# Output projection in units of 512 columns, from weight blocks of half the channel blocks

## The reference, cut to what matters

```python
h   = layer_norm(x) * (1 + sc1) + sh1
# mixer: attention and SSD branches, then
merged = sigmoid(g_a) * (attn @ w_attn_o) + sigmoid(g_b) * (y @ w_ssd_o)
mix    = merged @ w_out                       # the output projection: 640x1024 @ 1024x1024
x  = layer_norm(ALPHA * x + g1 * mix, ln1_g, ln1_b)
h  = layer_norm(x) * (1 + sc2) + sh2
ff = square(relu(h @ w_mlp1 + b_mlp1)) @ w_mlp2 + b_mlp2
x  = layer_norm(ALPHA * x + g2 * ff, ln2_g, ln2_b)
```

## Time and profile before

| | us |
|---|---|
| median of 3 runs | 1561.07 (1559.13 to 1561.4) |
| the profiled execution's own time | 1560.75 |
| its span, first to last instruction | 1559.1 |
| output projection on PE, from its first matmul to its last one's start | 1055.96 to 1115.27 |
| PE's wait before the MLP | to 1118.15 |

### The profile page before, as it was taken

One profiled execution on the slowest core, in us unless ns is written; L12 is line 12 of the kernel. 1 busy time (PEld: TensorE's weight loads), 2 busy tenths in 40 slices (PEclk: granted clock), 3 DMA queues, 4 the chain that ended last, 5 costly groups with the idle time before them and its releaser, 6 DMA issues.

```text
span 1559.1 us, 25181 instructions
## 1 busy us (share of the span) xinstructions
PE 1502.1 (96%) x10114; PEld 1394.2 (89%) x10114; DVE 1021.0 (65%) x1407; ACT 689.6 (44%) x1258; POOL 220.5 (14%) x230
## 2 busy tenths in 40 slices
PE   4999999999999989899999999999999999999997
PEld 2899999999999989898866799999998898998986
DVE  5666666658565688988876453346966773653768
ACT  2443343343564266777766443233532262451540
POOL 1011122100101100000000000000000541522720
PEclk9999999999999999999999999999999999999999
DMA  9555555543677777787630355335212122131241
GB/s 317 181 177 192 180 184 184 181 138 112 211 247 243 270 222 223 256 262 226 221 125 1 115 183 169 132 115 190 95 55 82 54 94 97 55 102 61 82 175 68
DMA packets 152511, 244.62 MB, mean 157 GB/s; under 512 B 8112, under 2 KB 110240, under 8 KB 149344
## 3 DMA queue, kind: packets, MB, share of 16 engines
q1 hardware_dynamic: 129232, 174.59, 33.5%
q0 software_dynamic: 12304, 47.72, 8.4%
q10 hardware_dynamic: 10880, 20.97, 5.2%
HBM read 196.63 MB, written 46.63 MB: 156 GB/s over the span
## 4 chain that ended last, share of the span: by engine, by line
PE 78%; DVE 13%; ACT 5%; DMA 1%; issue 1%; SPq 1%; ACTq 0%; DVEq 0%
PE acc L965 57%; PE tp L965 17%; ACT arena L1922 2%; DVE wlo L2288 1%; PE tp L1432 1%; DVE arena L2562 1%; DMA arena<-in_w_mod 1%; PE tp L1093 1%; DVE arena L2393 1%; ACT whi L1700 1%; DMA arena<-decay_sums_t 1%; DVE arena L2563 1%; ACT whi L2080 1%; DVE wlo L2763 1%; PE tp L1479 1%
## 5 line engine op out<-in xcount | busy, mean ns | idle before, releaser
L965 PE MATMUL acc<-hh,whi 128*128 128x322 f32 (+1 forms) x1068 | 287.0, 317 | 5.0 <-issue 3.0
L965 PE MATMUL acc<-hl,whi 128*128 128x322 f32 (+1 forms) x1068 | 280.6, 311 | 0.0
L965 PE MATMUL acc<-hh,wlo 128*128 128x322 f32 (+1 forms) x1068 | 279.9, 311 | 0.0
L965 PEld LDWEIGHTS acc<-hh,whi 128*128 128x128 f32 x1068 | 188.2, 189 | 9.7 <-issue 7.3
L965 PEld LDWEIGHTS acc<-hl,whi 128*128 128x128 f32 x1068 | 189.6, 189 | 0.0
L965 PEld LDWEIGHTS acc<-hh,wlo 128*128 128x128 f32 x1068 | 189.4, 189 | 0.0
L965 PE MATMUL acc<-whi,hh 128*128 128x256 f32 x640 | 183.1, 286 | 0.0
L965 PE MATMUL acc<-whi,hl 128*128 128x256 f32 x640 | 179.8, 281 | 0.0
L965 PE MATMUL acc<-wlo,hh 128*128 128x256 f32 x640 | 179.7, 281 | 0.0
L2288 DVE TENSOR_TENSOR wlo<-raw,whi 128x2048 fp32r<-128x2048 f32 x62 | 145.0, 2338 | 35.2 <-ACT whi L1700 35.2
L1700 ACT ACTIVATE whi<-raw 128x2048 fp32r<-128x2048 f32 x62 | 118.3, 1908 | 71.4 <-PE tp L965 48.3
(11 more groups left out here) (366 smaller groups left out, 3137.9 us busy)
## 6 DMA issues: line engine op xcount, KB each, us to landing
raw<-in_w_in SPq DMA_DIRECT2D x38, 1024.0 KB, 8.8
raw<-in_w_mlp SPq DMA_DIRECT2D x32, 1024.0 KB, 5.2
arena<-in_w_mod SPq DMA_DIRECT2D x24, 1024.0 KB, 8.3
arena<-decay_sums_t ACTq DMA_DIRECT2D x40, 512.0 KB, 6.0
arena<-xs_nat SPq DMA_DIRECT2D x8, 1024.0 KB, 10.7
raw<-in_w_ssd_o SPq DMA_DIRECT2D x8, 1024.0 KB, 6.6
y_nat<-arena POOLq DMA_DIRECT2D x6, 1024.0 KB, 7.5
arena<-y_nat SPq DMA_DIRECT2D x6, 1024.0 KB, 6.6
```

The costliest lines, as they stand in the source:

```text
L965: return pe.matmul(out, l, r, start=first, stop=last)
```

## The change

`w_out` comes in four blocks of 4 channel blocks by 512 columns, of the same 1024 KB (`wide` gives the view of a slot in that form). A unit is a tile by 512 columns, `OUT` lists (tile, column half, offset, columns), and `OUT_BANK` the `acc` bank. There are 11 units: tiles 0, 1 and 2 by the first column half, run as two passes over four channel blocks each; the same tiles by the second half; tile 3 and tile 4 by both, the last unit in two parts of 256 columns. `TURN` has tile 0 after unit 5, tile 1 after unit 7, tile 2 after unit 9. The first MLP block's split waits for unit 8, the last that uses `whi`.

```diff
-        U_MLP = U_OUT + 4 * NT
+        N_OUT = 2 * NT + 1
+        U_MLP = U_OUT + N_OUT
...
-        TURN = {10: 0, 14: 1, 17: 2}
+        OUT = [(t, 0, 0, 2 * BW) for t in range(3)] + [(t, 1, 0, 2 * BW) for t in range(3)]
+        OUT += [(3, 0, 0, 2 * BW), (3, 1, 0, 2 * BW), (4, 0, 0, 2 * BW), (4, 1, 0, BW), (4, 1, BW, BW)]
+        OUT_BANK = (0, 1, 2, 3, 0, 1, 2, 3, 0, 1, 3)
+        TURN = {5: 0, 7: 1, 9: 2}
...
-            stream(2, w_out, 0)
+            for c in range(2):
+                for b in range(2):
+                    step(lo)
+                    sp.wait_ge(lo["sem"], value(lo, 2))
+                    sp.dma_start(wide(raw, b), w_out[:, b * HK:(b + 1) * HK, c * 2 * BW:(c + 1) * 2 * BW]).then_inc(raws[b]["sem"], step(raws[b]))
...
+            def out_products(i, b):
+                t, c, at, n = OUT[i]
+                wh, wl = (wide(w, b) for w in ((whi, wlo), (w2h, w2l))[c])
+                for k in range(HK):
+                    kk = b * HK + k
                     if i == 0:
-                        pe.wait_ge(s["merge_ok"], k + 1)
...
+                        pe.wait_ge(s["merge_ok"], kk + 1)
+                    for m, w in ((hh, wh), (hh, wl), (hl, wh)):
+                        last = mul(acc[:, OUT_BANK[i], 0:n], m[:, kk, tok(t):tok(t) + P], w[:, k, at:at + n],
+                                   kk == 0 and w is wh and m is hh, kk == KT - 1 and m is hl)
                 return last
...
+            for b in range(2):
+                pe.wait_ge(lo["sem"], due(lo))
+                for i in range(3):
+                    if b == 0:
+                        step(free)
+                        pe.wait_ge(s["acc_free"], U_OUT - 1 + i // 2)
+                    last = out_products(i, b)
+                    if b:
+                        last.then_inc(ready["sem"], step(ready))
+            for i in range(3, N_OUT):
                 step(free)
...
+                pe.wait_ge(s["acc_free"], U_OUT + (0, 1, 2, 3, 4, 5, 6, 8)[i - 3])
+                for b in range(2):
+                    if i == 3:
+                        pe.wait_ge(lo["sem"], due(lo))
+                    last = out_products(i, b)
+                last.then_inc(ready["sem"], step(ready))
                 if i in TURN:
                     turn_tile2(TURN[i])
...
-                    act.wait_ge(ready["sem"], U_OUT + 17)
+                    act.wait_ge(ready["sem"], U_OUT + 9)
                     split_hi(0)
...
-                    act.wait_ge(ready["sem"], U_OUT + 18)
+                    act.wait_ge(ready["sem"], U_OUT + 9)
                     split_hi(1)
...
-            gated_out(4)
+            gated_out(1)
             summed(0)
-            gated_out(1)
             normed_once(0)
             gated_out(1)
             normed_twice(0)
             summed(1)
+            normed_once(1)
             gated_out(1)
-            normed_once(1)
-            gated_out(2)
             for t in range(2, NT - 1):
                 lower(t - 2)
                 normed_twice(t - 1)
                 summed(t)
-                gated_out(2)
+                gated_out(1)
                 normed_once(t)
-                gated_out(2 if t == 2 else 1)
+                gated_out(1)
             lower(2)
             split_lo(0)
             gated_out(1)
```

More of the change, by code:

```diff
@@ L436, in build @@
         GATED = {8 + 2 * q: q for q in range(4)}
-        OUT = [(0, 0), (1, 0), (2, 0), (0, 1), (1, 1), (0, 2), (0, 3), (1, 2), (1, 3), (2, 1), (2, 2), (2, 3)]
-        OUT += [(t, b) for t in range(3, NT) for b in range(4)]
-        TURN = {10: 0, 14: 1, 17: 2}
+        OUT = [(t, 0, 0, 2 * BW) for t in range(3)] + [(t, 1, 0, 2 * BW) for t in range(3)]
+        OUT += [(3, 0, 0, 2 * BW), (3, 1, 0, 2 * BW), (4, 0, 0, 2 * BW), (4, 1, 0, BW), (4, 1, BW, BW)]
+        OUT_BANK = (0, 1, 2, 3, 0, 1, 2, 3, 0, 1, 3)
+        TURN = {5: 0, 7: 1, 9: 2}
         LAST = [(t, c, 0, 2 * BW) for t, c in ((0, 0), (1, 0), (2, 0), (3, 0), (0, 1), (1, 1), (2, 1), (3, 1), (4, 0))]
@@ L1501, in _ @@
                     t_pass(1, sub, sub, yh, yl, KT, False, True).then_inc(ready["sem"], step(ready))
-            blocks = [(whi[:, 0], wlo[:, 0]), (whi[:, 1], wlo[:, 1]), (w2h[:, 0], w2l[:, 0]), (w2h[:, 1], w2l[:, 1])]
             def turn_tile2(t):
@@ L1511, in turn_tile2 @@
                 last.then_inc(s["h2_turned"], 1)
-            def out_products(i, ks):
-                t, b = OUT[i]
-                for k in ks:
+            def out_products(i, b):
[3 more added lines that the diff above has]
+                    kk = b * HK + k
                     if i == 0:
-                        pe.wait_ge(s["merge_ok"], k + 1)
-                    for m, w in ((hh, 0), (hh, 1), (hl, 0)):
-                        last = mul(acc[:, i % 4, 0:BW], m[:, k, tok(t):tok(t) + P], blocks[b][w][:, k],
-                                   k == 0 and w == 0 and m is hh, k == KT - 1 and m is hl)
-                return last
@@ L1523, in out_begun @@
[L1523 to L1527, removed]
-                step(free)
[L1529 to L1536, removed]
@@ L1537, in _ @@
-            for i in range(2, 4 * NT):
-                out_begun(i, seen)
-                out_products(i, range(KT)).then_inc(ready["sem"], step(ready))
+                        pe.wait_ge(s["merge_ok"], kk + 1)
+                    for m, w in ((hh, wh), (hh, wl), (hl, wh)):
+                        last = mul(acc[:, OUT_BANK[i], 0:n], m[:, kk, tok(t):tok(t) + P], w[:, k, at:at + n],
+                                   kk == 0 and w is wh and m is hh, kk == KT - 1 and m is hl)
+                return last
@@ L1664, in _ @@
                 if n < 2:
-                    pe.wait_ge(s["acc_free"], U_OUT + 4 * NT - 3 + 2 * n)
+                    pe.wait_ge(s["acc_free"], U_OUT + (9, 7)[n])
                 if n == 3:
@@ L1671, in _ @@
                 if n == 2:
-                    pe.wait_ge(s["acc_free"], U_OUT + 4 * NT)
+                    pe.wait_ge(s["acc_free"], U_MLP)
                     turn_tile2(NT - 1)
@@ L2836, in gated_out @@
                 for i in range(units["k"], units["k"] + n):
-                    t, b = OUT[i]
-                    cols = slice(b * BW, (b + 1) * BW)
+                    t, c, at, n_ = OUT[i]
+                    cols = slice(c * 2 * BW + at, c * 2 * BW + at + n_)
                     dve.wait_ge(ready["sem"], due(ready))
-                    dve.tensor_tensor(x1[:, t, cols], acc[:, i % 4, 0:BW], g1r[:, min(t, 1), cols], ALU.mult).then_inc(free["sem"], step(free))
+                    dve.tensor_tensor(x1[:, t, cols], acc[:, OUT_BANK[i], 0:n_], g1r[:, min(t, 1), cols], ALU.mult).then_inc(free["sem"], step(free))
                 step(units, n)
```

## The result

| | before | changed |
|---|---|---|
| median of 20 runs, us | 1561.07 (1559.13 to 1565.54) | 1563.62 (1562.74 to 1565.84) |
| ratio, 95% interval | 1 | 1.0017 (1.0012 to 1.0023) |
| span of the profiled run, us | 1559.1 | 1561.9 |
| from the start of the output projection on PE to the turning of tile 2 | 52.88 | 55.23 |
| ... to the first matmul of the MLP | 62.19 | 64.52 |

The changed kernel is 2.55 us slower, where 2.4 were forecast. The last three rows are distances in us within one trace, since the stage starts at 1056.30 in the changed kernel's and at 1055.96 in that of before.

The account below looks back on a forecast made before the run. PE's matmul stream was taken to bound the kernel; matmuls -0.71, fourth-block wait +0.3 and cover lost behind tile 2's turning +2.83 gave +2.4 us on 1561.07, so 1563.5 us, range 1561.0 to 1565.4.

Parts of the forecast that it names:

- The matmuls: Output projection on PE: 216 wide matmuls replace 432 narrow ones, 55.93 us for 56.64, a gain of 0.71 us.
- The start: First passes of the output projection: second block's low part is ready in time, new load form costs nothing, no wait.
- The fourth block: Unit 3: low part queued on DVE behind three evictions; PE stops 0.37 plus 0.1 us, net +0.3 us.
- The end of the stage: Tile 2 turned 2.4 us later, same 9.31 us of links, PE waits 5.4 us instead of 2.6 before the MLP.
- the lost cover: Behind tile 2's turning PE has one narrow unit instead of two, so the wait grows by 2.83 us.
- DVE in time: DVE's layer norms from summed(0) to lower(2) need 38.1 us, leaving 0.3 to 0.4 us of slack before the MLP.
- The clock: half_unit(0) after the wait: low clock costs some 1.7 us before; the same cost was taken for the changed kernel.
- the low clock lasts longer: Rival, half_unit(0) and half_unit(1): clock recovers later after the 5.4 us wait; +3.7 us, 1564.8 us; chance 0.28.
- The 0.9: Up to tile 4's turning: the shift is 2.4 - 0.9 us if the low clock falls wholly into the longer wait.
- The sum: Whole kernel: +2.4 us on the median 1561.07 gives 1563.5 us, 0.15% slower.

Follow-up runs that it names:

- e_width_fill: Changed kernel with each 512-column matmul issued as two of 256 and the wait before the MLP filled with 34 added matmuls; +2.05 us over before.
- e_low_fill: Changed kernel with the fourth block's low part on DVE ahead of unit 2's eviction, and 35 added matmuls filling the wait; +0.55 us over before.
- b_turn18: Kernel before with tile 2 turned after unit 18 instead of 17; +3.45 us over before.
- e_turn8: Changed kernel with tile 2 turned after unit 8 instead of 9; +2.61 us over before.
- e_low: Changed kernel with the fourth block's low part on DVE ahead of the eviction of unit 2 instead of behind it; +2.95 us over before.
- b_fill: Kernel before with 17 unused matmuls of 320 columns added between unit 19 and half_unit(0) to fill the wait; -1.27 us against before.
- b_best: Kernel before with the MLP's first four half units running high-part products first, turnings reordered, second block's low part later on DVE; -1.27 us against before.
- a_pool: Changed kernel with the first two MLP blocks' low parts on GpSimd, first high part earlier on ACT, fourth block's low part before unit 2's eviction; +3.63 us over before.
- b_pool: Kernel before with the first two MLP blocks' low parts on GpSimd instead of DVE and the first block's high part earlier on ACT; +2.48 us over before.

## Why the prediction was right

By its own steps. **The matmuls:** a gain of 0.71 us forecast, 0.81 to 0.83 measured by e_width_fill. **The start:** no wait for the second block, as forecast, and none for the first in its new form: PE's timeline has no pause from the end of the work before until unit 3. **The fourth block:** a stop of 0.47 forecast, 0.46 in the trace, and e_low_fill gives it back. The forecast's 0.37 is 0.05 more than its own times 1075.51 and 1075.83 give; in the trace PE did start 0.06 us behind the end of the low part. **The end of the stage:** tile 2 is turned 2.35 us later for 2.4 forecast, the links behind it take 9.29 us for 9.31, the wait is 5.42 for 5.4. b_turn18 gives the same wait by the order alone, so the lost cover, and not the new form of the units, makes it. **DVE in time:** 0.3 to 0.4 us of slack forecast, 0.18 in the trace, since DVE needed 38.26 us from summed(0) to the end of lower(2) (1079.98 to 1118.24) and not 38.1. e_turn8 confirms that there was no more: with the turning 1.38 us sooner the start gained 0.29. This was the step with least room. With another 0.2 us on DVE the number would have been right all the same, but by another chain. **The clock:** taken as unchanged. In the result's profile it was (5.01 us for half_unit(0) and 5.12 before). In general it isn't: longer low stretches are seen after the longer wait, and e_low's half_unit(0) of 6.34 us is what the rival "the low clock lasts longer" had named (6.4). Which of the two the median would follow the forecast had only weighed (0.50 against 0.28), so that it came to +2.55 and not to the rival's +3.7 is in part luck. The cost of the low clock in half_unit(0) before was forecast as 1.7 us and is 1.54 by b_fill (5.12 less 3.58). Of it 1.06 us was said to be all that the turning of tile 4 could come sooner; b_fill gained 1.04. The 0.9 that the forecast then took for it has no working.

**The sum:** +2.4 forecast, +2.33 at the MLP's start, +2.21 at the second half units, +2.55 in the medians. That the medians come so close to the traces is luck as well, since their interval is 1.7 us wide. Of the 2.8 us between the two profiled spans 0.34 lie ahead of the stage and some 0.25 behind the second half units; neither place was tested, and both are within what runs of one kernel differ by (the changed kernel's other 19 runs lie 0.9 below to 2.2 above the profiled one).

## What to carry to other kernels

A wait that the chain of waits calls "issue" can be read backwards over the engines to the instruction that begins its chain. What counts then is how much work the waiting engine has behind that instruction, so that regrouping this work into larger units can lengthen the wait by more than the larger units save. Where a product is split into parts, look whether PE waits for the low part while the matmuls with the high part, two thirds of the work here, could run: in b_best's trace the wait went from 2.60 to 0.27 us, though the times don't show its gain clear of none.

## What the runs showed of the hardware that I had not expected

A GpSimd `tensor_tensor` of two SBUF inputs over 128x2048 (4.60 us) kept DVE's `scalar_tensor_tensor` on SBUF, begun 0.4 us after it, from finishing until 1.09 us after its own end: 5.29 us instead of 1.28; in a_pool 5.32, and the second pair cost DVE 3.28 and 3.29 instead of 1.28. In all four cases DVE's end came 1.08 or 1.09 us after GpSimd's, while DVE's `bn_stats` in the middle of the second one (b_pool, from 1120.75) took its usual 1.29 us for two. So these two instructions did not slow each other by a share: DVE's had to wait for nearly all of the other. And the same kernel, with the same wait of 5.4 us, had its clock low for 3.3 us in one profile and for 6.9 us in another.
